# Differential attention: q filler by length of step, new key tiles, and norms of six heads beside the last head

## The reference, cut to what matters

```python
def diff_attn_mixer(h, w_in, lam_vecs, subln_w, w_out, cos, sin, layer):
    q, k, v = jnp.split(h @ w_in, 3, axis=-1)
    q = apply_rope(q.reshape(B, L, 8, 2, 64), cos, sin)
    k = apply_rope(k.reshape(B, L, 8, 2, 64), cos, sin)
    v = v.reshape(B, L, 8, 128)
    # lam from lam_vecs
    o = causal_diff_attention(q, k, v, lam)     # softmax(q0 k0) v - lam * softmax(q1 k1) v
    o = rmsnorm(o, subln_w, SUBLN_EPS) * (1.0 - lam_init)   # per token and head, over 128
    return o.reshape(B, L, D_MODEL) @ w_out
```

## Time and profile before

| what | us |
|---|---|
| median of three runs | 3167.83 (3162.16 to 3170.81) |
| the profiled execution, its span | 3170.47, 3168.3 |
| PE busy over the span | 2891.9 (91%) |
| attention from the first q block to od_out | 2563.22 to 2728.09 |
| scores of a step start | 2566.09 (n=0), 2568.39, 2571.39, 2575.10, 2580.51 (n=4) ... 2651.22 (n=20), 2654.78, 2658.87, 2663.09 ... 2668.50 (n=24), 2673.63, 2677.71, 2681.40, 2687.06 (n=28), 2690.80, 2694.98, 2697.77 |
| ACT ends the exponentials of steps 20, 21, 29, 30, 31 | 2653.48, 2657.72, 2694.54, 2698.62, 2703.04 |
| ACT ends keep(27) | 2695.16 |
| DVE ends the maximum of step 30, PE the scores of step 31 | 2697.32, 2699.49 |
| a table load; the Sqrt of 32 sums | 1.28; 0.32 |
| high part of a head (2816); low part (2899); spread (2895) | 0.69; 0.75; 0.68 |
| the eight matmul instructions of one head (2767) | 1.16 |
| weight high part (363); weight low part (354) | 1.05; 2.4 to 2.9 |
| od_out: last matmul of tile 0 starts; tile 0 squared and stored by ACT; high part of unit 2 | 2733.50; 2733.93 to 2735.02; 2734.91 to 2735.97 |
| SP's next two weight loads, issued together at 2728.74 | 5.89 |

### The profile page before, as it was taken

How to read it: one execution, slowest core, us unless ns; L and a number is a source line. 1 busy time by engine, 2 the same in 40 slices (tenths; PEclk the granted TensorE clock), 3 DMA queues, 4 the chain that set the end, 5 groups by cost and what they waited for, 6 DMA issues and landing times. The chain is left out here.

```text
span 3168.3 us, 44970 instructions
## 1 busy us (share of the span) xinstructions
PE 2891.9 (91%) x17926; PEld 2359.0 (74%) x17926; DVE 1404.2 (44%) x2250; ACT 995.5 (31%) x1521; POOL 1075.5 (34%) x751
## 2 busy tenths in 40 slices
PE   6888699999899989998989888899998998889997
PEld 4576367677688668787768876799998866768885
DVE  5788245520205611302038676281443536383352
ACT  2222253322212236423225332222123545332221
POOL 0332022344333159544433320044442321234442
PEclk9999899999999999999999997999999999999999
DMA  3888111134473259422222100122222210122222
GB/s 132 263 265 253 42 53 41 60 130 153 150 219 105 99 126 260 143 96 80 86 85 74 42 3 2 60 87 93 88 93 68 87 54 21 54 73 93 94 98 73
DMA packets 130750, 324.86 MB, mean 103 GB/s; under 512 B 54144, under 2 KB 54784, under 8 KB 129808
## 3 DMA queue, kind: packets, MB, share of 16 engines
q1 hardware_dynamic: 96128, 221.90, 21.6%
q0 software_dynamic: 30096, 88.21, 9.8%
q10 hardware_dynamic: 4352, 12.26, 1.0%
HBM read 288.32 MB, written 33.95 MB: 102 GB/s over the span
## 5 line engine op out<-in xcount | busy, mean ns | idle before, releaser
L354 POOL TENSOR_TENSOR ring_r<-ring,high 128x1024 fp32r<-128x1024 f32 x327 | 822.5, 2515 | 1452.1 <-ACT high L363 1452.1
L261 PE MATMUL ps<-h_hi,high 128*128 128x512 f32 (+1 forms) x2104 | 737.9, 359 | 52.0 <-POOL ring_r L354 22.2
L266 PE MATMUL ps<-h_hi,ring_r 128*128 128x512 f32 (+1 forms) x2104 | 664.0, 350 | 0.0
L264 PE MATMUL ps<-h_r,high 128*128 128x512 f32 (+1 forms) x1912 | 646.3, 347 | 0.0
L363 ACT ACTIVATE high<-ring 128x1024 fp32r<-128x1024 f32 x359 | 379.9, 1058 | 822.8 <-PE ps L261 692.2
L261 PEld LDWEIGHTS ps<-h_hi,high 128*128 128x128 f32 x2104 | 401.3, 191 | 130.2 <-issue 59.6
L266 PEld LDWEIGHTS ps<-h_hi,ring_r 128*128 128x128 f32 x2104 | 371.6, 191 | 54.2
L264 PEld LDWEIGHTS ps<-h_r,high 128*128 128x128 f32 x1912 | 366.2, 192 | 41.8 <-issue 1.4
L264 PE MATMUL ps<-f_r,high 128*128 128x264 f32 (+1 forms) x832 | 261.2, 326 | 0.0
L261 PE MATMUL ps<-f_hi,high 128*128 128x264 f32 (+1 forms) x768 | 236.6, 321 | 0.0
L261 PE MATMUL ps<-z_hi,high 128*128 128x512 f32 x488 | 196.9, 403 | 19.5 <-POOL ring_r L354 13.6
(11 more groups left out here) (458 smaller groups left out, 4313.6 us busy)
## 6 DMA issues: line engine op xcount, KB each, us to landing
ring<-in_units SPq DMA_DIRECT2D x402, 512.0 KB, 3.3
d_ca<-arena POOLq DMA_DIRECT2D x16, 640.0 KB, 8.8
arena<-d_ca POOLq DMA_DIRECT2D x16, 640.0 KB, 7.1
arena<-d_q POOLq DMA_DIRECT2D x32, 256.0 KB, 8.0
d_pb<-arena POOLq DMA_DIRECT2D x16, 512.0 KB, 10.6
arena<-d_pb POOLq DMA_DIRECT2D x16, 512.0 KB, 4.2
arena<-d_ca POOLq DMA_DIRECT2D x16, 512.0 KB, 5.0
arena<-d_k POOLq DMA_DIRECT2D x128, 64.0 KB, 4.1
```

Source lines behind the costliest of these rows:

```text
L261: part = mm(acc, hi[:, cols], self.x_hi(k)[:, t0:t0 + tn], start=(k == 0), stop=False)
L264: mm(acc, hi[:, cols], self.x(k)[:, t0:t0 + tn], start=False, stop=False)
L266: ins = mm(acc, w[:, cols], self.x_hi(k)[:, t0:t0 + tn], start=False, stop=(k == self.kt - 1))
L354: eng.tensor_tensor(b.ring_r[:, slot, :], b.ring[:, slot, :], self.high[:, (j + self.flip) % 2, :], ALU.subtract).then_inc(b.unit_lo, 1)
```

## The change

1. The filler has 1, 1, 2, 4 k-blocks in the steps of tau 0, 1, 2, 3, and six blocks lie ahead of step 0. It still ends at step 25.
2. The key tiles are (0, 72), (72, 72), (144, 128), (272, 128), (400, 128): they end where query tiles end. v is computed and stored in these tiles.
3. The last head uses banks 0 and 1 alone, with the wait of the other heads.
4. Heads 0 to 5 are normed in the last head: a Sqrt at n = 29 and a reciprocal at n = 30 for 24 sums, spreads at n = 30, 31, 32 (two heads each), the matmuls and the high and low parts one step later, in banks 2 and 3. Heads 6 and 7 have a Sqrt of their own.
5. The high parts of od_out's units 0 and 1 are made at n = 32, their low parts ahead of the last squares. od_out begins with blocks 0 to 5 of tiles 0 and 1, then come the matmuls of heads 6 and 7, then blocks 6 and 7 of both tiles. Unit 1 raises `begun` at its block 6.

```diff
+        self.given, self.split, self.amid = 1, None, None
         def feature_major(it):
-            for o in range(self.body_outs):
+            pieces = 2 if self.split and it == 0 else 0
+            for o in range(pieces):
+                one_out(o, it, range(self.split))
+            if pieces:
+                self.amid(pe)
+            for o in range(pieces):
+                one_out(o, it, range(self.split, self.kt))
+            for o in range(pieces, self.body_outs):
                 one_out(o, it)
         def one_out(o, it, ks=range(self.kt)):
+            begun_at = self.split if self.split and first and o == 1 else 0
-                            if k % 8 == 0 and t0 == 0:
+                            if k % 8 == begun_at and t0 == 0:
                                 part.then_inc(b.begun, 1)
...
-KEY_TILES = [(META + t * P, P) for t in range(4)] + [(0, META)]
+NEAR = (META + P) // 2
+KEY_TILES = [(0, NEAR), (NEAR, NEAR)] + [(META + t * P, P) for t in range(1, 4)]
+Q_BLOCKS = (1, 1, 2, 4)
+EARLY = 6
...
+        self.early = {self.steps - 2 + i: (2 * i, 2 * i + 1) for i in range(EARLY // 2)}
     def tensor(self, pe):
-        for n in range(0, 4, 2):
-            self.query_tile(pe, n)
+        self.query_blocks(pe, 0, 6)
...
-                    pe.wait_ge(self.powered, 2 * n - (2 if n > LAST_HEAD else 0))
+                    pe.wait_ge(self.powered, 2 * n)
...
-                self.query_tile(pe, 4 + 2 * n)
+                self.query_blocks(pe, 6 + 8 * h + sum(Q_BLOCKS[:tau]), Q_BLOCKS[tau])
+            if n - 1 in self.early:
+                for h in self.early[n - 1]:
+                    self.head(pe, h, 2 + h % 2)
...
+    def head(self, pe, h, bank):
+        pe.wait_ge(self.spread, h + 1)
+        if 2 <= h < EARLY:
+            pe.wait_ge(b.out_lo, self.at["parts"] + h - 1)
+        for t in range(4):
+            ins = b.nc.tensor.matmul(b.ps[:, bank, t * P:(t + 1) * P], m.o[:, h, t, :], m.spread[:, h % 2, t, :],
+                                     start=True, stop=True)
+        ins.then_inc(self.headed, 1)
...
     def scalar(self, act):      # in the loop over n, behind power, keep, high_unit and shift
+            if n == self.steps - 3:
+                self.root(act, 0, EARLY)
+            if n == self.steps:
+                self.feeds.make_high(act, 0, 0, free=True)
+                self.feeds.make_high(act, 1, 0, free=True)
+            for h in self.early.get(n - 1, ()):
+                self.keep_head(act, h)
+        self.root(act, EARLY, DIFF_HEADS)
+        for h in range(EARLY, DIFF_HEADS):
+            self.keep_head(act, h)
...
     def gpsimd(self, pool):
             self.q.g.low_unit(pool, h + 2)
+            if h == DIFF_HEADS - 1:
+                self.feeds.low_unit(pool, 0)
+                self.feeds.low_unit(pool, 1)
             squares(h)
...
     def vector(self, dve):      # in the loop over n, behind keep_out, top, join, combine and sum_squares
+            if n == self.steps - 2:
+                inverse_roots(0, EARLY)
+            for h in self.early.get(n, ()):
+                spread(h)
+            for h in self.early.get(n - 1, ()):
+                low_part(h)
         sum_squares(DIFF_HEADS - 1)
+        inverse_roots(EARLY, DIFF_HEADS)
+        for h in range(EARLY, DIFF_HEADS):
+            spread(h)
+        for h in range(EARLY, DIFF_HEADS):
+            low_part(h)
     def feed(self, gemm):
         gemm.ready, gemm.fed, self.feeds = self.ready, True, gemm
+        gemm.given, gemm.split, gemm.amid = 2, EARLY, self.last_heads
```

More of the change, by code:

```diff
@@ L431, in body @@
                 first = isinstance(it, int) and it == 0
-                if not (self.fed and first and j == 0) and not (self.late and first and j < 2):
+                if not (self.fed and first and j < self.given) and not (self.late and first and j < 2):
                     self.make_high(act, j, it)
@@ L2677, in __init__ @@
         b.norms["squared"] += 2 * DIFF_HEADS
[L2678 to L2679 removed]
+        b.norms["rooted"] += 2
+        b.norms["inverted"] += 2
         b.norms["parts"] += DIFF_HEADS
@@ L2687, in parts @@
         h, tau = divmod(n, 4)
-        tiles = [(META + i * P, P) for i in range(tau + 1)] + [(0, META)]
-        return h, tau, META + tau * P, META + (tau + 1) * P, tiles
+        return h, tau, META + tau * P, META + (tau + 1) * P, KEY_TILES[:tau + 2]
     def turned_to(self, j, i, kn):
@@ L2727, in tensor @@
                 meta = [b.ps[:, 6, META * c:META * (c + 1)] for c in range(2)]
-                to = [b.ps[:, self.score_bank(n) + c, 0:main] for c in range(2)]
+                to = [b.ps[:, c, 0:main] for c in range(2)]
                 if first:
@@ L2755, in tensor, with head_bank, last_heads @@
                 for i, (k0, kn) in enumerate(tiles):
-                    of = i if kn == P else 4
                     ins = mm(b.ps[:, 7, tau * P:(tau + 1) * P], m.prob_t[0:kn, j % 2, i * P:(i + 1) * P],
-                             m.v[0:kn, of, h * P:(h + 1) * P], start=(i == 0), stop=(i == len(tiles) - 1))
+                             m.v[0:kn, i, h * P:(h + 1) * P], start=(i == 0), stop=(i == len(tiles) - 1))
                 ins.then_inc(self.mixed, 1)
[L2760 to L2769, removed]
+    def head_bank(self, h):
+        return 2 + h % 2 if h < EARLY else 4 + h % 2
+    def head(self, pe, h, bank):
+        b, m = self.b, self.m
+        pe.wait_ge(self.spread, h + 1)
[5 more added lines that the diff above has]
+        ins.then_inc(self.headed, 1)
+    def last_heads(self, pe):
+        for h in range(EARLY, DIFF_HEADS):
+            self.head(pe, h, self.head_bank(h))
     def scalar(self, act):
@@ L2809, in scalar, with root, keep_head @@
                 self.q.shift(act, n // 4)
[L2810 to L2814, removed]
-            act.wait_ge(self.turned, self.steps + h + 1)
-            f(m.o_hi(h), b.ps[:, 4 + h % 4, :], ACT.Copy, scale=sub).then_inc(b.out_hi, 1)
+            if n == self.steps - 3:
[8 more added lines that the diff above has]
+            self.keep_head(act, h)
+    def root(self, act, first, last):
+        b, m = self.b, self.m
+        act.wait_ge(b.squared, self.at["squared"] + 2 * last)
+        b.nc.scalar.activation(m.roots[:, 4 * first:4 * last], m.squares[:, 4 * first:4 * last], ACT.Sqrt,
+                               bias=b.eps[1e-5], scale=1.0 / P).then_inc(b.rooted, 1)
+    def keep_head(self, act, h):
+        b, m = self.b, self.m
+        act.wait_ge(self.headed, h + 1)
+        b.nc.scalar.activation(m.o_hi(h), b.ps[:, self.head_bank(h), :], ACT.Copy, scale=b.col("od_subln_w_2", 0)
+                               ).then_inc(b.out_hi, 1)
     def gpsimd(self, pool):
```

51 lines of the change are left out of this document (26 added, 25 removed).

## The result

The changed kernel takes 3149.18 us (median of 5 runs, 3145.66 to 3156.21) against 3167.83 for the kernel before (5 runs, 3162.16 to 3179.13): ratio 0.9941, 95% interval 0.9915 to 0.9967. That is a gain of 0.6%, small but clear of the noise. A second comparison of the same kernel, in 12 runs, gave 3154.17 against 3165.93: 0.9962, 0.9946 to 0.9978. The gain is 12 to 19 us, where 2.8 was forecast.

A forecast was written before the change was run, and what follows sets the result against it. It took TensorE (PE), busy 91% of the span, as the bound. Heads with their clock -7.7 us and tail +4.9 (-2.5 + 7.4) gave -2.8 from the profiled 3170.47, or 3165 from the median; range 3156 to 3174.

The forecast's parts named there:

- The clock in the tail: Last head to od_out's unit 2: new PE waits bring the clock down; 0 to +10.6 us possible, +7.4 taken.
- the walk at full clock: Last head to od_out's unit 2, timed without clock falls: unit 2 starts at 2736.8 against 2739.31, a gain of 2.5 us.
- The walk through the last head: PE waits ahead of step 31's scores, heads 2, heads 4 and unit 2: 1.6, 2.1, 3.1 and 3.3 us.
- Key tiles were priced at 0: Two key tiles of 72 rows replace 128 and 16: matmul counts and spacing stay, weight loads hidden, so 0 us.
- Filler: Blocks 1, 1, 2, 4 in attention steps: -1.29 us a steady head, -6.1 us up to the last head with both ends.
- the slack of 0.2 us: In tau 2 of steady heads PE still decides, ending at 7.63 against 7.4 for ACT's exponentials.
- The clock in the heads: Heads 1 to 5 lose their idle gaps, so one of two slow steps goes: 1.57 us; head 0's 1.6 us stays.
- the clock holds: Rival: the clock stays up through the tail, -7.7 - 2.5 = -10.2 us, 3157.6; chance 0.25.
- ACT bounds tau 2: Rival: ACT bounds tau 1 and 2 of the heads, losing 0.5 us more per head, 3 us, so 3168; chance 0.10.
- The serial slow tail: Rival: from step 31's scores to od_out one serial loop at half clock, +11 us, 3172.7 in all; chance 0.17.
- The switches at the page's price: Rival: two added ACT table switches in the last head also drain, step 30's exponentials 2.8 us later, 3168; chance 0.03.
- A reading: From the profile page: outside the attention stage PE's matmuls follow one another without a gap; PE busy 91% of the span.

The follow-up runs named there:

- heads first: Changed kernel, with ScalarE making the high parts of heads 2 and 3 ahead of the two weight high parts in step 32: ratio 0.9962 to the kernel before.
- the four versions with other orders: Changed kernel with heads 2 and 3 ahead of weights, od_out tile 1 split at block 3, that plus unit 2 before evacuation, or all: 0.9962, 0.9944, 0.9943, 0.9935.

## Why the prediction was wrong

Forecast was a gain of 2.8 us, found 14 in the profiles. Of the 11 us between (forecast from the first scores to unit 2: -2.8 - 1.36 = -4.2; measured 173.22 to 158.07 = -15.2), the tail has 7.2 and the heads 3.8.

- **The clock in the tail is the step that failed**: "I take 0.7 of 10.6 [...] +7.4". The tail was forecast at -2.5 + 7.4 = +4.9 and came out at -2.3 (52.25 to 49.99), and at -2.1 in the second profile; against the same 52.25 with the tiles left as they were it came out at +0.2 (52.45). The waits were 1.5 us longer than walked in sum and the stretch up to step 31's scores 0.5 shorter (11.77 against 10.71 + 1.6), so no net slowing is left. Compared directly, the slow clock behind step 31's scores cost 2.6 us, not 7.4. It lies between heads 4 and 5 and blocks 6 of od_out, here in the changed kernel and then in the one with heads first, where the same instructions ran at full clock:

```profile
2700.85:2719.12 18.27, 17.51 (x92) 15.71 (x92) 6.05 (x11) 4.88 (x8) 3.33 (x2) 0.84 0.09 30
```

```profile
2688.27:2703.97 15.70, 14.94 (x91) 13.04 (x92) 6.05 (x11) 6.42 (x10) 5.72 (x3) 1.00 0.11 33
```

The other stretches behind those scores (7.15, 6.49 and 6.31 us) took as long in other profiles at 1.00. (The second run of the changed kernel loses 3.2 us this way, 1.7 of it ahead of heads 2 and 3.) So 4.8 of the 7.2 us are this term, 1.8 the walk at full clock (37.4 us forecast from step 31's scores to unit 2, 38.2 - 2.6 measured), and 0.5 the stretch ahead of it. The term's bounds, 0 to 10.6, held it; the choice between them was wrong. It took the longer waits for the stronger reason, but the clock stayed at 2.4 GHz over 12.29 us that begin behind a wait of 1.53 and hold one of 2.83, and fell only at 2699.7, for 7 us. The rows of before had shown as much: four gaps of 1.3 us without a fall, and two with one. A wait makes a fall possible; how likely it is could not be read from one profile. Over the five profiles of kernels that keep these gaps (1.3 to 1.5 us, six each) it fell behind 4 of 30.
- **The walk through the last head named the right waits**: forecast 1.6, 2.1, 3.1, 0 and 3.3 us, measured 1.53, 2.83, 3.36, 0.76 and 3.15. The parts of heads 6 and 7 were not wholly hidden. That the first came out so near is partly luck of the clock's course, since the second run has 2.21 and 1.59 for the first two. The work between the waits was forecast too long; the four mixes, 0.19 us shorter each by the tiles, are 0.8 us of it at most; where the rest lies stays open.
- **Key tiles were priced at 0, bounds -0.5 to +1, and gave 0.58 us a head alone**: three steps of 0.19, 4.8 us in the tiles' own comparison (0 to 9.5), outside the bounds. The rows of weight loads were read for the duration of an instruction. What it costs to come to it from one of another height lay in the mix of before, 1.02 us for six matmuls, and shows only beside the changed kernel's 0.83.
- **Filler**: 15.9 a head alone, forecast 15.99; steps 2.86, 3.41, 4.20, 5.43 against 2.88, 3.41, 4.22, 5.47. First scores +1.27 against +1.36, head 0 14.40 against 14.5. With the tiles in, PE's tau 2 is short enough for the slack of 0.2 us to be used up: 4.14 with 0.06 idle, and tau 3 is the chain of 5.41. So beside the filler the tiles save 0.19 + 0.20 + 0.06 + 0.02 a head. With the 0.09 by which the filler's head was priced too long, that is 0.56 a head, 2.8 over heads 1 to 5.
- **The clock in the heads**: the slow step of head 6 went, as forecast, and that of head 1 too (18.85 to 15.42), which the prediction left in: 1.6 us. In exchange the clock falls in step 27 of head 6 now, in the changed kernel and its repeat (16.58 and 16.56 us): head 6 was forecast at 15.8, 0.8 less. In the four versions with other orders, whose code is the same up to there, it does not fall, and head 6 takes 15.42 or 15.43. 2.8 + 1.6 - 0.8 are the 3.8 of the heads, to 0.2. The profile of before was an unlucky one in this: at 4 falls in 30, its six gaps would cost 1.3 us on average (an estimate), not the 3.1 of its two falls.
- **The rivals**: "the clock holds" (-10.2, 3157.6) was nearest in its mechanism, though the clock did not hold all the way (0.86 over the tail). ACT bounds tau 2 indeed, but by 0.06 us instead of 0.5. The serial slow tail did not come: ACT's and DVE's orders made the waits as walked, not longer. The switches at the page's price, 1.38 us of drain each by the Trainium skill, "ScalarE: Activation LUTs", section "What ACT_TABLE_LOAD costs", are not borne out: no drain, and 0.5 us for both here, 1.2 in the second run, where the sum had 0.7.
- **A reading**: that PE has no gap outside the attention stage is not so. It is busy for 2315 of the first 2540 us; the row shown holds for its own 15 us. Nothing in the sum rests on it.

The median fell by 18.7 us, 4 more than the profiles; the second comparison has 11.8. That spread is of the runs: with the same code up to there, the first scores start at 2551.7 to 2566.1 us in kernels with the code of before, and at 2555.9 to 2570.0 with that of the changed one.

## What to carry to other kernels

Where one profile shows the clock falling behind some waits and not behind equal ones, a longer wait elsewhere is no price by itself: carry both ends, and look for the price in runs, since the same tail with the same tiles took 52.3 to 55.9 us here. A change of the tiles' heights can pay by itself: count how often TensorE's stationary operand changes between short and tall, and order or cut the tiles so that this is seldom. Filler belongs where the step has a wait that other engines set, and when it is used up, matmuls that nobody reads keep the clock up too. In the kernel before they brought 0.23%, in the changed kernel nothing that the time tells.

## What the runs showed of the hardware

- A change of the stationary operand's rows between short (16 or 64) and tall (72 or more) costs TensorE 0.19 us (steps of 2.67, 2.86 and 3.05 us with none, one and two more). That 16 and 64 differ as well is inferred from the count.
- Of TensorE's clock: behind a wait of 1.53 us, and over one of 2.83, it stayed at 2.4 GHz for 12.29 us with PE busy 7.45 of them; behind one of 2.55 us it was at 1.2 GHz for part or nearly all of the next 10.71 and 13.75 us (0.68, 0.51) with PE busy throughout, and with that wait filled the stretch ran at 1.00. A microsecond at 1.2 GHz costs 0.45 when PE is busy throughout (7.61 us against 10.71 and 13.75).
- Two table loads and a root between two exponentials take 2.93 us (2682.97 to 2685.90) and cost PE 0.5 to 1.2 (step 30 takes 4.18 to 4.86 us against 3.69 without the loads).
